# A first weight split by VectorE, low-rank squares added on VectorE, a score order moved by three tiles and a last pair on GpSimd

## What is computed

```
h   = rms_norm(x, g)                          # 256 x 1024
a   = h @ w_a                                 # -> ckv (256), cq (384), key rope (64)
q   = rms_norm(cq) @ w_uq ; kv = rms_norm(ckv) @ w_ukv ; rope on 64 columns
s   = (q k^T + q_rope k_rope^T) * scale ; p = softmax(mask(s)) ; o = p v ; y = o @ w_o
...                                           # feed-forward, two more layers
out = rms_norm(x, g_final)
```

## Time and profile before

| | us |
|---|---|
| three runs | 960.72, 961.36, 961.59 (median 961.36) |
| the profiled execution, its own time | 960.99 |
| its span (first to last instruction) | 959.1 |
| PE busy | 944.2 |
| DVE busy | 718.9 |
| ACT busy | 543.6 |
| POOL busy | 17.8 |

### The profile page before, as it was taken

How to read it: one execution, slowest core, us unless ns; L and a number is a source line. 1 busy time by engine, 2 the same in 40 slices (tenths; PEclk the granted TensorE clock), 3 DMA queues, 4 the chain that set the end, 5 groups by cost and what they waited for, 6 DMA issues and landing times.

```text
span 959.1 us, 18737 instructions
## 1 busy us (share of the span) xinstructions
PE 944.2 (98%) x7890; PEld 911.9 (95%) x7890; DVE 718.9 (75%) x1332; ACT 543.6 (57%) x845; POOL 17.8 (2%) x51
## 2 busy tenths in 40 slices
PE   9999999999999999999999999999999999999997
PEld 9989999999998988899999998998999999999996
DVE  7875897787569777799888789655656789888653
ACT  7755654444447366565444554556756576766542
POOL 0000000000000000000000000000320000000000
PEclk9999999999999999999999999999999999999999
DMA  9645487667736734268768892653344636555621
GB/s 341 231 169 206 166 281 249 233 251 270 256 134 220 263 132 139 83 224 314 295 227 290 317 329 75 258 176 133 107 143 147 220 132 220 183 213 179 217 89 44
DMA packets 28259, 195.62 MB, mean 204 GB/s; under 512 B 3216, under 2 KB 3600, under 8 KB 5264
## 3 DMA queue, kind: packets, MB, share of 16 engines
q1 hardware_dynamic: 28176, 194.43, 57.3%
HBM read 192.98 MB, written 1.05 MB: 202 GB/s over the span
## 4 chain that ended last, share of the span: by engine, by line
PE 93%; ACT 3%; DVE 2%; DMA 1%; issue 1%; SPq 0%; POOL 0%; DVEq 0%; ACTq 0%
PE bank L548 26%; PE bank L549 25%; PE bank L554 25%; PE bank L750 2%; PE bank L776 2%; PE bank L592 2%; PE bank L603 2%; PE bank L597 1%; PE bank L760 1%; PE bank L631 1%; PE bank L637 1%; PE bank L632 1%; PE bank L669 1%; PE bank L675 1%; PE bank L670 1%; DMA s_front<-in_front 1%
## 5 line engine op out<-in xcount | busy, mean ns | idle before, releaser
L1507 DVE TENSOR_TENSOR s_wlo<-s_raw,s_whi 128x512 fp32r<-128x512 f32 (+1 forms) x354 | 364.4, 1070 | 121.9 <-ACT s_whi L1017 121.7
L1017 ACT ACTIVATE s_whi<-s_raw 128x1024 fp32r<-128x1024 f32 (+2 forms) x226 | 299.5, 1353 | 193.6 <-PE bank L554 187.3
L548 PE MATMUL bank<-s_hh,s_whi 128*128 128x256 f32 x1392 | 390.2, 280 | 1.3 <-DVE s_wlo L1507 1.0
L549 PE MATMUL bank<-s_hl,s_whi 128*128 128x256 f32 x1392 | 384.8, 276 | 0.0
L554 PE MATMUL bank<-s_hh,s_wlo 128*128 128x256 f32 x1383 | 382.2, 276 | 0.0
L548 PEld LDWEIGHTS bank<-s_hh,s_whi 128*128 128x128 f32 x1392 | 261.4, 188 | 6.6 <-issue 4.2
L549 PEld LDWEIGHTS bank<-s_hl,s_whi 128*128 128x128 f32 x1392 | 261.5, 188 | 0.1
L554 PEld LDWEIGHTS bank<-s_hh,s_wlo 128*128 128x128 f32 x1383 | 259.7, 188 | 0.0
L548 PE MATMUL bank<-s_ph,s_whi 128*128 128x256 f32 x528 | 145.9, 276 | 0.0
L549 PE MATMUL bank<-s_pl,s_whi 128*128 128x256 f32 x528 | 145.7, 276 | 0.0
L554 PE MATMUL bank<-s_ph,s_wlo 128*128 128x256 f32 x525 | 144.9, 276 | 0.0
(11 more groups left out here) (274 smaller groups left out, 1288.6 us busy)
## 6 DMA issues: line engine op xcount, KB each, us to landing
s_raw<-in_gu SPq DMA_DIRECT2D x44, 1024.0 KB, 5.0
s_raw<-in_dn SPq DMA_DIRECT2D x33, 1024.0 KB, 4.9
s_raw<-in_wada SPq DMA_DIRECT2D x24, 1024.0 KB, 5.2
s_raw<-in_up SPq DMA_DIRECT2D x22, 1024.0 KB, 4.9
s_raw<-in_wo SPq DMA_DIRECT2D x8, 1024.0 KB, 4.9
s_raw<-in_win_g SPq DMA_DIRECT2D x8, 1024.0 KB, 4.9
s_raw<-in_mla SPq DMA_DIRECT2D x4, 1024.0 KB, 13.9
s_raw<-in_wkv_v SPq DMA_DIRECT2D x4, 1024.0 KB, 5.7
```

The lines of the kernel that those rows point to most:

```text
L548: e.matmul(out, hi, xh[:, k, :], start=first, stop=False, skip_group_check=True)
L549: e.matmul(out, hi, xl[:, k, :], start=False, stop=False, skip_group_check=True)
L1017: e.activation(whi[w % SPLIT][:, at], src, ACT.Copy).then_inc(S.hi.tick((w, c0)), 1)
L1507: e.tensor_tensor(wlo[s][:, at], src, whi[s][:, at].bitcast(F32), ALU.subtract).then_inc(S.lo.tick((i, j), (i, "all")), 1)
```

## The change

Five edits, in the program's order.

1. VectorE makes the high part of the first four tiles (`tensor_copy`), and ScalarE skips it. 
2. VectorE makes two quarters of the low part of the third piece (w = 2) two and three steps earlier, ahead of the last two `angle` steps; ScalarE makes the second half of its high part ahead of the sines.
3. The low-rank squares (two terms for kv, three for q) are added by VectorE (`low_squares_added`), so that TensorE has one matmul with ones for each, not two and three.
4. ScalarE copies the rope rows of the query ahead of the table load, with two high halves ahead of it; and `PAIR0` goes from 18 to 21 for the pairs 0 and 1.
5. At the end the scale is also written to a PSUM bank, from which VectorE multiplies three of the four pairs; GpSimd multiplies the fourth (tiles 4 and 5) from SBUF, and the DMAs go out in the order 0, 2, 6, 4.

```diff
-PAIR0 = (18, 18, 44, 44)
+PAIR0 = (21, 21, 44, 44)
...
-            for j in range(0, 8, 2):
-                q.wait_ge(S.result, j)
+            for j in (0, 2, 6, 4):
+                q.wait_ge(S.pool_result if j == 4 else S.result, j)
                 e.dma_start(a["out"][:, j:j + 2, :], yb[:, j:j + 2, :]).then_inc(S.out_stored.tick(j), 16)
...
-                q.wait_ge(S.square, (s, "all"))
                 q.wait_ge(S.sqsum, ("x0", "sum"))
-                terms = [(ones, src) for src in low_squares[s]] + [(shares[s], sqacc[0][:, 0:T])]
-                for i, (fixed, src) in enumerate(terms):
-                    m = e.matmul(out[:, 0:T], fixed[:, :], src, start=i == 0, stop=True, skip_group_check=True)
-                m.then_inc(S.sums.tick(s), 1)
+                e.matmul(out[:, 0:T], shares[s][:, :], sqacc[0][:, 0:T], start=True, stop=True, skip_group_check=True)
+                q.wait_ge(S.sqsum, (s, "low"))
+                e.matmul(out[:, 0:T], ones[:, :], low_squares[s][0], start=False, stop=True, skip_group_check=True).then_inc(
+                    S.sums.tick(s), 1)
...
             for k in range(8):
                 x_high(k)
-                hi_part(2)
+                if k == 0:
+                    parts.pop(0)
+                else:
+                    hi_part(2)
...
             hi_part(3)
+            hi_part(3)
+            x0_square(2)
             q.wait_ge(S.rot, "angle")
...
-            x0_square(2)
             q.wait_ge(S.trig, "abs")
             e.activation(cosb, tmp[0][:, :], ACT.Sin, scale=-1.0, bias=epsc[:, 1:2]).then_inc(S.trig.tick("cos"), 1)
-            hi_part(3)
...
-            log_tables()
+            hi_part(5)
             hi_part(5)
             q.wait_ge(S.gemm, ("wuq", 0))
             e.activation(A0.Q[:, 8:10, :], pair(banks[bank_of["wuq", 0]]), ACT.Copy).then_inc(S.rope_raw.tick("query"), 1)
-            hi_part(5)
+            log_tables()
...
+            e.activation(banks[7][:, 0:T], logs[:, 0:T], ACT.Exp, scale=-0.5).then_inc(S.rms.tick("x6"), 1)
+            e.activation(Rs[0][:, 0:T], logs[:, 0:T], ACT.Exp, scale=-0.5).then_inc(S.rms.tick("x6 again"), 1)
...
+            def low_squares_added(s):
+
+                terms = low_squares[s]
+                q.wait_ge(S.square, (s, "all"))
+                for src in terms[1:]:
+                    q.wait_latest(S.sqsum)
+                    e.tensor_tensor(terms[0], terms[0], src, ALU.add).then_inc(S.sqsum.tick((s, "low")), 1)
...
+            q.wait_ge(S.first_in[0], 0)
+            e.tensor_copy(whi[0][:, 0:4 * P], first_w[:, 0, :]).then_inc(S.hi0.tick("first"), 1)
             for k in range(8):
                 x_low(k)
                 lo_part(2)
                 if k >= 2:
                     angle(k - 2)
+            lo_part(3)
+            lo_part(3)
             angle(6)
             angle(7)
             square_sum("x0", 1, sqv[1])
             lo_part(3)
             lo_part(3)
             square_sum("x0", 2, sqv[2])
-            lo_part(3)
-            lo_part(3)
...
             fold("x0")
+            lo_part(5)
+            lo_part(5)
+            for s in ("kv", "q"):
+                low_squares_added(s)
             for _ in range(4):
                 lo_part(5)
-            lo_part(5)
-            lo_part(5)
...
-            for j in range(0, 8, 2):
+            for j in (0, 2, 6):
...
+            q.wait_ge(S.rms, "x6 again")
+            q.wait_ge(S.act_out, ("result", 5))
+            e.tensor_tensor(yb[:, 4:6, :], xT[:, 4:6, :], Rs[0][:, 0:T].rearrange("p (a b) -> p a b", a=1).broadcast_to([P, 2, T]),
+                            ALU.mult).then_inc(S.pool_result.tick(4), 1)
```

More of the change, by code:

```diff
@@ L437, in build @@
         S.hi = signal("weight_high_made")
+        S.hi0 = signal("first_weight_high_made")
         S.xhi = signal("x_high_made")
@@ L460, in build @@
         S.result = signal("result_made")
+        S.pool_result = signal("result_made_by_gpsimd")
         R_OF = {"x0": 0, "kv": 1, "q": 2, "y0": 0, "x1": 1, "z0": 2, "x2": 0, "y1": 1, "x3": 2, "z1": 0, "x4": 1,
@@ L515, in sync_program @@
                     e.dma_start(bias2[:, :, :], a["relm"]).then_inc(S.relm_in.tick("relm"), 16)
-            for j in range(0, 8, 2):
-                q.wait_ge(S.result, j)
+            for j in (0, 2, 6, 4):
+                q.wait_ge(S.pool_result if j == 4 else S.result, j)
                 e.dma_start(a["out"][:, j:j + 2, :], yb[:, j:j + 2, :]).then_inc(S.out_stored.tick(j), 16)
-            q.wait_ge(S.out_stored, 6)
+            q.wait_ge(S.out_stored, 4)
         def tensor_program(e, counted):
@@ L537, in weight @@
                 part = next(i for i, (lo, hi) in enumerate(_lo_parts(w)) if lo <= c < hi)
-                if high:
+                if high and w == 0 and c < 4:
+                    q.wait_ge(S.hi0, "first")
+                elif high:
                     q.wait_ge(S.hi, (w, c))
@@ L1478, in scalar_program @@
                 result_scaled(j)
-            rms("x6")
+            q.wait_ge(S.sums, "x6")
+            e.activation(logs[:, 0:T], banks[bank_of["sums", "x6"]][:, 0:T], ACT.Ln, scale=1.0 / D,
+                         bias=epsc[:, 0:1]).then_inc(S.act_tmp.tick(("log", "x6")), 1)
+            q.wait_ge(S.act_tmp, ("log", "x6"))
+            e.activation(banks[7][:, 0:T], logs[:, 0:T], ACT.Exp, scale=-0.5).then_inc(S.rms.tick("x6"), 1)
+            e.activation(Rs[0][:, 0:T], logs[:, 0:T], ACT.Exp, scale=-0.5).then_inc(S.rms.tick("x6 again"), 1)
         def vector_program(e, counted):
@@ L1505, in lo_part @@
                 src = first_w[:, 4 * i + j, :] if i < 2 else raw[p % RAW][:, at]
-                q.wait_ge(S.hi, (i, c[1] - 1))
+                if (i, j) == (0, 0):
+                    q.wait_ge(S.hi0, "first")
+                else:
+                    q.wait_ge(S.hi, (i, c[1] - 1))
                 e.tensor_tensor(wlo[s][:, at], src, whi[s][:, at].bitcast(F32), ALU.subtract).then_inc(
@@ L2123, in vector_program @@
             q.wait_ge(S.resid, ("x6", 6))
-            twice = Rs[0][:, 0:T].rearrange("p (a b) -> p a b", a=1).broadcast_to([P, 2, T])
-            for j in range(0, 8, 2):
+            twice = banks[7][:, 0:T].rearrange("p (a b) -> p a b", a=1).broadcast_to([P, 2, T])
+            for j in (0, 2, 6):
                 q.wait_ge(S.act_out, ("result", j + 1))
```

## The result

The changed kernel takes 966.42 us, median of 4 runs (966.18 to 966.71), beside 961.28 for the kernel before (4 runs, 960.72 to 961.59): ratio 1.0055, 95% interval 1.0043 to 1.0067. It is slower by 5.1 us.

A forecast was written before the change was run, and what follows sets the result against it. TensorE, busy nearly the whole span, was taken as the bound. -1.74 + 2.6 + 1.04 + 0.5 - 0.1 = +2.3 us on 960.99 gave 963.3, stated as 963.4; own range 962.3 to 964.8, 8-in-10 range 960.7 to 964.9.

The forecast's parts named there:

- Edit 1: First tiles' high parts on VectorE: 0, since warm-up loads keep TensorE busy until 6.07; at most 0.5 us without that cover.
- Edit 2: Third piece sooner: TensorE's w = 2 wait goes, 1.2 us gained; w = 3's second high half comes late, 0.4 given back.
- Edit 3: Low-rank squares added on VectorE: three of eight matmuls go, 1.30 us gained on TensorE.
- They are free only because of edit 4: VectorE's adds, 1.26 us, cost nothing only because the table load moves behind ScalarE's high halves, ending VectorE's 1.22 us idle time.
- The lead at `wuv`: Start of `wuv`: 1.74 us sooner, of the head's 2.5; VectorE's K rows, which free bank 0, keep the rest.
- Edit 4, turn (0, 0): Scores moved 18 to 21: serial path of 12.8 us from `wuv`'s start; TensorE waits some 2.7 us, loss 2.6.
- The clock is out, since the granted clock is full: Whole kernel: the clock cannot move the end, so no term for it was put in the sum.
- First `wo0` tile: Behind turn (1, 0): three units less cover TensorE's wait, 1.04 us more; bounds 0.7 to 1.1.
- Tile 16: Tile 16 of `wo0`, needing chunk 1: 0.69 us less cover against 0.17 of slack, 0.5 lost; bounds 0 to 0.7.
- Edit 5, the tail: Last output pairs and stores: 0.1 us gained, bounds 0 to 0.4, since DMA transfers bound the stores.
- the third: Head: w = 2's low quarter still late or bank 0 freed at the old time, losses in full; 964.5 to 965; chance 0.06.
- The first rival: Head's gain arrives: ScalarE and VectorE finish in time for turn (0, 0), nothing lost there; -1.5, 959.5; chance 0.12.

The follow-up runs named there:

- a later base: Pairs 0 and 1's scores at 19 instead of 18, on the changed kernel with old order and key-copy bank release (959.73 us): 959.59 us.

## Why the prediction was wrong

The direction was right, and the order is the cause of the loss, as forecast; the size was not: +2.3 forecast, +5.6 in the profiled execution, above the range. Two things make the missing 3.3 us: the head's lead of 1.74, which did not reach `wuv`, and the clock, which the sum left out. Step by step:

- **Edit 1: 0.** Nothing in the traces speaks against it; it wasn't run alone.
- **Edit 2: 1.2 gained, 0.4 given back.** The wait is gone, and 0.16 us is given back at the next low quarter, less than forecast. But the first product of w = 2 starts at 17.63 and not at 17.1, mostly because the products ahead of it followed each other at 0.118 us where they did at 0.113 before. The sums start at 26.98 instead of 27.56: 0.58 net, 0.8 forecast.
- **Edit 3: 1.30 gained on TensorE, the step that failed.** The products did go (sums over near 29.1), but TensorE then waited 1.47 for the bank of `wuq` unit 6, which the key rope's first product frees. The prediction even had the key rope's time (30.1 forecast, 30.30 measured) and wrote that TensorE would be 2.1 sooner, but named no place where TensorE waits for the key rope. In the kernel before the tie was hidden: the rope's first product was over at 30.97 and TensorE arrived at 31.02. The two runs with edit 3 alone show it: without the bank's release 0.1 us, which is nothing, with it 0.9. "They are free only because of edit 4" was wrong as well: the additions fitted without it.
- **The lead at `wuv`: 1.74.** Measured 0.04. Besides the wait, another 0.2 went between 30.77 and 41.37, where the products again followed each other at 0.118 us and not at 0.113. This isn't the change's doing: the kernel with ten filling products runs the same program up to there, shows 0.113, and starts `wuv` at 40.96. With the bank freed early the lead is 1.93, held by VectorE's K rows, the gate that the prediction named, and within its bounds; the median fell by 1.6. So the bank accounts for 1.7 of the missing 3.3.
- **Edit 4, turn (0, 0): 2.6.** Right. Path 12.75 against 12.8, wait 2.54 against 2.7, and a loss of 54.12 - 50.62 - 1.04 = 2.46 behind a `wuv` that started as before. It was also right that a lead does not help: 2.54 stayed 2.54 when the bank was freed early. Not right was the query rope's end, 35.9 forecast: it waited 0.70 for its halves and ended at 36.75. That cost nothing, since scores 0 came at 38.30.
- **Not in the sum: the clock.** "The clock is out, since the granted clock is full" was true of the kernel before and was taken over unasked to a kernel in which TensorE stands still for 2.7 us. That cost 1.51 us in the profiled execution and 1.6 in the median (966.42 against 964.78 with the wait filled), the other half of the missing 3.3.
- **First `wo0` tile: +1.04.** Right: the wait went from 0.38 to 1.44, 1.06. **Tile 16: +0.5.** Right: 0.43.
- **Edit 5, the tail: 0.1 gained.** Nothing measured, alone or at the end. The pair on GpSimd was ready in time. The 1.28 us that it took lies in the bounds of 0.5 to 2.1 and near the 1.1 taken; the estimate of 1.1 to 1.3 from the Trainium skill (GPSIMD Engine Reference, Elementwise) holds. The stores went on as before, at 364 to 404 GB/s, and did not reach the 436 by which up to 0.4 us was to be had.

With the measured terms: -0.04 + 2.46 + 1.51 + 1.06 + 0.43 + 0.05 = 5.47, of 5.6 between the spans. Nothing of size is left over.

The rival that came true in part is the third: the change does not do in the head what it says. It had 0.06 and 964.5 to 965; with the clock on top of it the result lay beyond it. The first rival counted idle times of 1.08 and 0.64 to "each of the two engines"; both are VectorE's, which changed nothing, as its path stayed serial. Since the forecast of a wait over 2.5 us stood in the text, the range should have asked what TensorE does after such a wait.

## What to carry to other kernels

When work is taken off an engine, follow that engine's next instructions to each of their semaphores, also those that hold a bank or a buffer and not data: one that fires just before the engine arrives shows no wait now and takes the whole gain later. If a bank is released by an instruction that doesn't read it, release it by the last that does; here three lines turned a gain of nothing into 0.9 us. And moving independent work ahead of a dependent pair by a few tiles can put the pair behind unrelated work in the other engines' in-order queues, so the place has to be judged there. Here 3 tiles cost 5.4 to 5.8 us, 1 tile on a later base nothing.

## What the runs showed of the hardware

- After 2.54 us without a product (51.6 to 54.1) TensorE worked at 1.2 GHz for some 3.2 us in the profiled execution of the changed kernel, and its three other executions took as long. With the same wait it stayed at 2.4 GHz in the profiled executions of the order alone and of the bank freed early; by time and mean clock, so did one more of the order alone (964.85 and 0.999 against 966.56 to 966.93 and 0.997). After 1.60 us of waiting it stayed there in the profiled execution, and none of the six lies apart. What decides it in one execution and not in the other was not tried.
- Ten products of 128x128 that nobody reads, put into the wait, kept the clock and with it 1.6 us. They cost nothing as long as they fit into the wait; 42 of them, 9.54 us, cost 5 us.
- The fp32 product of 128x128 used as filling takes 0.227 us as two instructions, while the kernel's weight products of twice the columns follow each other at 0.12 us.
- With the granted clock at 1.00 throughout, the same products follow each other at 0.118 us in one execution and at 0.113 in another. Between 31 and 38 us it was 0.118 in the profiled executions of the changed kernel and of scale 0 ahead of the low quarter, and 0.113 in those of the two filled waits, whose program is the same up to there. Over the 63 products there that is nearly 0.3 us. What sets it stays open.
- On GpSimd a two-input multiplication of 128x512 took 1.28 us; VectorE's pairs beside it took 0.63 each, as before (1.88 for three, 2.50 for four).
